# Experts of a mixture-of-experts stage in pairs, with high and low pieces stacked as rows of one stationary operand

## The reference, cut to what matters

```
g_sel = argmax(g_logits)                  # one of 4 groups a token
top_v, top_i = top_k(e_in, 2)             # two of its 8 experts
expert_idx = g_sel * 8 + top_i            # 256 * 2 = 512 assignments to 32 experts
hb = silu(xb @ w_g[e]) * (xb @ w_u[e])    # 1024 -> 512, twice
y = hb @ w_d[e]                           # 512 -> 1024
out[token] += y * gate
```

## Time and profile before

| what | value |
|---|---|
| median of 3 runs | 2004.26 us (2004.13 to 2004.6) |
| the profiled execution's own time | 2002.97 us |
| its span | 2001.2 us |
| PE busy | 1889.1 us (94%), 9124 matmuls |
| DVE busy | 1336.1 us (67%) |
| ACT busy | 1053.1 us (53%) |
| weights loaded by SP's queue | 423.87 MB in 400 transfers |
| experts' stage, from its first matmul to the last combining one | 257.9 to 858.3 us |

### The profile page before, as it was taken

The page is one execution under the profiler, slowest core; times in us unless marked ns, Lnnn a source line. Parts: engine busy times, 40 slices in busy tenths (PEclk is TensorE's granted clock), DMA queues, the critical chain, the costliest instruction groups (busy, mean ns, idle before and its releaser), DMA issues.

```text
span 2001.2 us, 22062 instructions
## 1 busy us (share of the span) xinstructions
PE 1889.1 (94%) x9124; PEld 1559.7 (78%) x9124; DVE 1336.1 (67%) x1263; ACT 1053.1 (53%) x1060; POOL 188.9 (9%) x171
## 2 busy tenths in 40 slices
PE   5998589999999999989999989999999999799998
PEld 4986467877787787768888978887888788587887
DVE  3776578888888888765546865555554668746554
ACT  3553367777877787644434354444443444335442
POOL 0001021111111110000000000000000108300000
PEclk9999789999999999989999999999999999899999
DMA  8744368999999999935546435555555667355551
GB/s 291 214 154 158 106 243 329 353 351 352 351 350 352 346 360 347 379 125 184 187 171 233 132 107 196 189 189 177 191 189 189 218 217 240 104 188 194 182 185 60
DMA packets 76219, 454.53 MB, mean 227 GB/s; under 512 B 16582, under 2 KB 17030, under 8 KB 24785
## 3 DMA queue, kind: packets, MB, share of 16 engines
q1 hardware_dynamic: 59024, 423.87, 58.3%
q0 software_dynamic: 16064, 27.51, 5.0%
q10 hardware_dynamic: 1024, 1.69, 0.3%
HBM read 461.49 MB, written 22.02 MB: 242 GB/s over the span
## 4 chain that ended last, share of the span: by engine, by line
PE 85%; DVE 7%; ACT 3%; POOL 2%; issue 2%; DMA 1%; SPq 0%; POOLq 0%; DVEq 0%; ACTq 0%
PE PS L422 27%; PE PS L424 26%; PE PS L423 26%; DVE wl L417 3%; ACT wh L408 2%; PE PS L1480 1%; PE PS L2013 1%; POOL vv L2633 1%; POOL vv L2635 1%; PE PS L1494 1%; DMA ring<-in_wt 1%; PE PS L2507 1%; DVE xg__148 L527 1%; DVE yTl L472 0%; PE PS L517 0%
## 5 line engine op out<-in xcount | busy, mean ns | idle before, releaser
L417 DVE TENSOR_TENSOR wl<-ring,wh 128x2048 fp32r<-128x2048 f32 x356 | 817.9, 2300 | 404.5 <-ACT wh L408 404.4
L408 ACT ACTIVATE wh<-ring 128x2048 fp32r<-128x2048 f32 x356 | 676.4, 1903 | 308.4 <-PE PS L424 307.0
L422 PE MATMUL PS<-wh,XTh 128*128 128x512 f32 x1048 | 418.3, 399 | 21.9 <-DVE wl L417 17.6
L424 PE MATMUL PS<-wh,XTl 128*128 128x512 f32 x1048 | 411.2, 392 | 0.0
L423 PE MATMUL PS<-wl,XTh 128*128 128x512 f32 x1048 | 411.1, 392 | 0.0
L422 PEld LDWEIGHTS PS<-wh,XTh 128*128 128x128 f32 x1048 | 198.8, 190 | 66.6 <-DVE wl L417 21.3
L424 PEld LDWEIGHTS PS<-wh,XTl 128*128 128x128 f32 x1048 | 198.5, 189 | 42.6
L423 PEld LDWEIGHTS PS<-wl,XTh 128*128 128x128 f32 x1048 | 198.9, 190 | 39.5
L422 PE MATMUL PS<-wh,xgT 128*128 128x512 f32 x388 | 159.1, 410 | 7.3 <-issue 2.9
L424 PE MATMUL PS<-wh,xgT 128*128 128x512 f32 x388 | 153.6, 396 | 0.0
L423 PE MATMUL PS<-wl,xgT 128*128 128x512 f32 x388 | 152.7, 394 | 0.0
(11 more groups left out here) (415 smaller groups left out, 2717.3 us busy)
## 6 DMA issues: line engine op xcount, KB each, us to landing
ring<-in_wt SPq DMA_DIRECT2D x400, 1024.0 KB, 5.1
xtmp<-in_norm_g POOLq DMA_DIRECT2D x6, 512.0 KB, 6.7
bb<-in_b_b_in POOLq DMA_DIRECT2D x12, 256.0 KB, 5.2
toep<-frow POOLq DMA_DIRECT2D x1, 2048.0 KB, 48.3
...
```

The lines of the kernel that those rows point to most:

```text
L408: s.activation(k.pieces(i)[0], k.raw(i), ACT.Copy).then_inc(*k.w_hi.up(i))
L417: v.tensor_tensor(l, k.raw(i), h.bitcast(F32), ALU.subtract).then_inc(*k.w_lo.up(i))
L422: pe.matmul(o, lhsT=left[0], rhs=right[0], start=first, stop=False)
L424: return pe.matmul(o, lhsT=left[1], rhs=right[0], start=False, stop=final)
```

## The change

Two experts share one gather of 64 + 64 tokens (`SEATS` = 64), one turning and one store. The turned tokens of an expert are laid out as 64 high columns and 64 low columns of one stationary operand, so that gate and up need two matmuls for each 128 rows of weights (by the high and by the low piece of the weights) where `three` took three: 32 an expert for 48. Rows 0 to 63 of the result hold the high tokens' product, rows 64 to 127 the low ones'. ACT copies the result to SBUF (`gs`, `us`), and four float32 matmuls of 64 moving columns with `fold` (two identities, one under the other) turn it and add its halves (`fold_gate`, `fold_up`). silu, the product `pr` and the pieces of h then have 256 columns for 512. The down product keeps three matmuls with 128 stationary columns, in which the other expert's 64 seats are zero, and both experts of a pair add up in the same PSUM banks (`down`, `rows`). The parts come in the order gate 0, gate 1, up 0, down 0, down 1 (of the expert before), up 1. Slots of a pair are made from ranks shifted by 512 for odd experts. `rest_*` now runs where an expert has over 64 tokens, in two rounds of 32.

```diff
     for e in range(32):
+        g = len(parts)
         cols("w_e_gate", (0, e), 0, 512)
+        u = len(parts)
+        cols("w_e_up", (0, e), 0, 512)
         if e:
             deep("w_e_down", (0, e - 1), 0, 4)
-        cols("w_e_up", (0, e), 0, 512)
+            parts.append(parts.pop(u + 1))
+            stage["down", e - 1] = (u + 1, u + 2)
+        stage["gate", e], stage["up", e] = (g, g + 1), (u, len(parts) - 1)
+    stage["down", 31] = (len(parts), len(parts) + 1)
     deep("w_e_down", (0, 31), 0, 4)
...
-        self.hsm = here("hsm", 8872, 512)
-        self.hrm = here("hrm", 9384, 512)
+        self.gs, self.us = here("gs", 8872, 512), here("us", 9384, 512)
+        self.sg, self.pr = here("sg", 9896, 256), here("pr", 10152, 256)
+        self.fold = here("fold", 10408, 64)
+        self.odp = here("odp", 8872, 4, 16)
...
-        self.xgT = [[here(f"xgT{x}{h}", 10672 + 2048 * x + 1024 * h, 8, 128, dtype=F32R) for h in T] for x in T]
+        self.xgT = [here(f"xgT{x}", 10672 + 2048 * x, 8, 2, 128, dtype=F32R) for x in T]
...
+    pe.wait_ge(*k.d["late"].at("late"))
     pe.wait_ge(*m.v.at("both"))
     for t in T:
+        pe.matmul(bank(0, 32, 32 * t), lhsT=k.ones, rhs=k.odd, start=True, stop=False)
...
-    def up_part(i, e, b, p):
+            for x in range(4):
+                o = 128 * (4 * q + x)
+                mm = pe.transpose(bank(6 + q, 128, 128 * x), k.xg[j % 2][:, o:o + 128], k.ident)
+            mm.then_inc(*m.pe.up(f"xt{j}.{q}g"))
+
+    def part(i, e, b, p):
         pe.wait_ge(*k.w_lo.at(i))
         w = k.weights(i)
         for j in range(4):
             kk = 4 * p + j
-            mm = rows_of(pe, bank(b), k.xgT[e % 2], kk, 0, w, j, 0, 512, kk == 0, kk == 7)
+            for n in T:
+                mm = pe.matmul(bank(b), lhsT=k.xgT[e // 2 % 2][:, kk, e % 2, :], rhs=w[n][:, j, :],
+                               start=(kk, n) == (0, 0), stop=(kk, n) == (7, 1))
         mm.then_inc(*k.w_used.up(i))
 
-    def turn_h(e):
-        pe.wait_ge(*m.v.at(f"pr{e}"))
+    def fold(src, b, name):
         for j in range(4):
-            mm = pe.transpose(bank(2, 128, 128 * j), k.hrm[:, 128 * j:128 * j + 128], k.ident)
-        mm.then_inc(*m.pe.up(f"ht{e}"))
-
-    def down(i, e, b):
+            mm = pe.matmul(bank(b, 64, 64 * j), lhsT=src[:, 128 * j:128 * j + 128], rhs=k.fold, start=True, stop=True)
+        mm.then_inc(*m.pe.up(name))
+
+    def fold_gate(e):
+        pe.wait_ge(*m.s.at(f"gs{e}"))
         if e:
-            pe.wait_ge(*m.s.at(f"yb{e - 1}"))
+            pe.wait_ge(*m.s.at(f"si{e - 1}"))
+        fold(k.gs, 2, f"fg{e}")
+
+    def fold_up(e):
+        pe.wait_ge(*m.s.at(f"us{e}"))
+        if e:
+            pe.wait_ge(*m.v.at(f"pr{e - 1}"))
+        fold(k.us, 3, f"fu{e}")
+
+    def down(e):
+
+        if e % 2 == 0 and e:
+            pe.wait_ge(*m.s.at(f"yb{e // 2 - 1}"))
         pe.wait_ge(*m.v.at(f"hl{e}"))
-        for p in range(2):
-            pe.wait_ge(*k.w_lo.at(i + p))
-            w = k.weights(i + p)
+        for p, i in enumerate(k.at["down", e]):
+            pe.wait_ge(*k.w_lo.at(i))
+            w = k.weights(i)
             for nn in range(2):
                 for j in range(2):
                     kk = 2 * p + j
-                    mm = rows_of(pe, bank(b + nn), k.hTm[e % 2], kk, 0, w, j, 512 * nn, 512 * nn + 512, kk == 0, kk == 3)
+                    mm = rows_of(pe, bank(4 + nn), k.hTm[e % 2], kk, 0, w, j, 512 * nn, 512 * nn + 512,
+                                 (e % 2, kk) == (0, 0), (e % 2, kk) == (1, 3))
                 if (e, p, nn) == (31, 1, 0):
                     mm.then_inc(*m.pe.up("y31"))
-            mm.then_inc(*k.w_used.up(i + p))
-
-    def combine(x, t, nn):
-        return pe.matmul(bank(4 + 2 * t + nn), lhsT=k.PT[:, x, 128 * t:128 * t + 128],
-                         rhs=k.yr[:, x, 512 * nn:512 * nn + 512], start=x == 0, stop=x == 1)
-
-    i = k.at["moe"]
+            mm.then_inc(*k.w_used.up(i))
+
     turn_x(0)
     for e in range(32):
+        g, u = k.at["gate", e], k.at["up", e]
+        if e % 2 == 0:
+            pe.wait_ge(*m.v.at(f"xl{e // 2}.1g"))
         if e:
-            pe.wait_ge(*m.s.at(f"si{e - 1}"))
-        pe.wait_ge(*m.v.at(f"xl{e}.1g"))
-        up_part(i, e, 0, 0)
+            pe.wait_ge(*m.s.at(f"gs{e - 1}"))
+        part(g[0], e, 0, 0)
         if e:
-            turn_h(e - 1)
-        up_part(i + 1, e, 0, 1)
-        i += 2
-        if e:
-            down(i, e - 1, 4)
-            i += 2
-            pe.wait_ge(*m.v.at(f"pr{e - 1}"))
+            fold_up(e - 1)
+        part(g[1], e, 0, 1)
         if e == 2:
             pe.wait_ge(*m.v.at("hotg"))
             for x in T:
                 for t in T:
-                    mm = pe.matmul(bank(3, 128, 256 * x + 128 * t), lhsT=k.ones, rhs=k.hotg[:, x, t, :], start=True,
+                    mm = pe.matmul(bank(6, 128, 256 * x + 128 * t), lhsT=k.ones, rhs=k.hotg[:, x, t, :], start=True,
                                    stop=True)
             mm.then_inc(*m.pe.up("gates"))
-        up_part(i, e, 1, 0)
-        if e < 31:
-            turn_x(e + 1)
-        up_part(i + 1, e, 1, 1)
-        i += 2
-    turn_h(31)
+        if e:
+            pe.wait_ge(*m.s.at(f"us{e - 1}"))
+        part(u[0], e, 1, 0)
+        if e:
+            down(e - 1)
+        if e % 2 and e < 31:
+            if e == 3:
+                pe.wait_ge(*m.v.at("PT1"))
+            turn_x(e // 2 + 1)
+        fold_gate(e)
+        part(u[1], e, 1, 1)
+    fold_up(31)
     pe.wait_ge(*m.v.at("PT1"))
-    pe.wait_ge(*m.s.at("yb30"))
-    for t in T:
-        for nn in T:
-            combine(0, t, nn)
-    down(i, 31, 2)
+    down(31)
     for t in T:
         for nn in T:
             if t == 0:
-                pe.wait_ge(*m.s.at(("ya31", "yb31")[nn]))
-            combine(1, t, nn).then_inc(*m.pe.up(f"c{t}.{nn}"))
+                pe.wait_ge(*m.s.at(("ya15", "yb15")[nn]))
+            pe.matmul(bank(COMBINED[2 * t + nn]), lhsT=k.PT[:, 128 * t:128 * t + 128],
+                      rhs=k.yr[:, 1, 512 * nn:512 * nn + 512], start=True, stop=True).then_inc(
+                *m.pe.up(f"c{t}.{nn}"))
...
+    def product(e):
+        v.wait_ge(*m.s.at(f"si{e}"))
+        v.wait_ge(*m.pe.at(f"fu{e}"))
+        if e:
+            v.wait_ge(*m.v.at(f"hl{e - 1}"))
+        v.tensor_tensor(k.pr, k.sg, bank(3, 256), ALU.mult).then_inc(*m.v.up(f"pr{e}"))
+
+    def low(e):
+        h, l = [seats(x, e) for x in k.hTm[e % 2]]
         v.wait_ge(*m.s.at(f"hh{e}"))
-        v.tensor_tensor(l, bank(2).rearrange("p (k i) -> p k i", k=4), h.bitcast(F32),
-                        ALU.subtract).then_inc(*m.v.up(f"hl{e}"))
-
-    i = k.at["moe"]
+        v.tensor_tensor(l, k.pr.rearrange("p (k i) -> p k i", k=4), h.bitcast(F32), ALU.subtract).then_inc(
+            *m.v.up(f"hl{e}"))
+
     turn_x(0)
     for e in range(32):
+        g, u = k.at["gate", e], k.at["up", e]
         if e:
-            turn_h(e - 1)
-        for n in range(4 if e else 2):
-            split_lo(v, k, k.after[i + n])
-        i += 4 if e else 2
-        if e < 31:
-            turn_x(e + 1)
-        split_lo(v, k, k.after[i])
-        v.wait_ge(*m.s.at(f"si{e}"))
-        v.wait_ge(*k.w_used.at(i + 1))
-        v.tensor_tensor(k.hrm, k.hsm, bank(1), ALU.mult).then_inc(*m.v.up(f"pr{e}"))
-        split_lo(v, k, k.after[i + 1])
-        i += 2
+            d = k.at["down", e - 1]
+            split_lo(v, k, k.after[k.at["up", e - 1][1]])
+            product(e - 1)
+        split_lo(v, k, k.after[g[0]])
+        if e:
+            low(e - 1)
+        split_lo(v, k, k.after[g[1]])
+        split_lo(v, k, k.after[u[0]])
+        if e:
+            for i in d:
+                split_lo(v, k, k.after[i])
+        if e % 2 and e < 31:
+            turn_x(e // 2 + 1)
+        if e == 0:
+            for h in T:
+                for x in T:
+                    v.memset(seats(k.hTm[x][h], 1 - x).bitcast(F32), 0.0).then_inc(*m.v.up(f"hz{x}{h}"))
+            v.wait_ge(*k.d["xn"].at("xn"))
+            v.memset(k.xg[1], 0.0).then_inc(*m.v.up("xz1"))
...
+    def gate(e):
+        s.wait_ge(*k.w_used.at(k.at["gate", e][1]))
+        if e:
+            s.wait_ge(*m.pe.at(f"fg{e - 1}"))
+        s.activation(k.gs, bank(0), ACT.Copy).then_inc(*m.s.up(f"gs{e}"))
+
+    def up(e):
+        s.wait_ge(*k.w_used.at(k.at["up", e][1]))
+        if e:
+            s.wait_ge(*m.pe.at(f"fu{e - 1}"))
+        s.activation(k.us, bank(1), ACT.Copy).then_inc(*m.s.up(f"us{e}"))
+
+    def silu(e):
+        s.wait_ge(*m.pe.at(f"fg{e}"))
+        if e:
+            s.wait_ge(*m.v.at(f"pr{e - 1}"))
+        s.activation(k.sg, bank(2, 256), ACT.Silu).then_inc(*m.s.up(f"si{e}"))
+
+    def high(e):
+        s.wait_ge(*m.v.at(f"pr{e}"))
+        if e >= 2:
+            s.wait_ge(*k.w_used.at(k.at["down", e - 2][1]))
+        s.activation(seats(k.hTm[e % 2][0], e), k.pr.rearrange("p (k i) -> p k i", k=4), ACT.Copy).then_inc(
             *m.s.up(f"hh{e}"))
 
```

(92 more changed lines are left out.)

255 lines of the change are left out of this document (110 added, 145 removed).

## The result

The changed kernel takes **1986.09 us** (median of 4 runs, 1984.77 to 1988.06) against 2004.43 for the kernel before in the same session; the ratio is 0.9906, with a 95% interval of 0.9889 to 0.9924. The forecast was 1992 with a range of 1966 to 2018. The profiled execution took 1984.77, its span is 1982.9.

What follows compares the result with a forecast made beforehand. PE was taken as the bound, DVE close behind. Loops -25, first loop -3, end 0 and clock falls +16 made -12 from 2002.97, so 1991; with the median 1.3 above that execution, forecast 1992 us, range 1966 to 2018.

Steps and rivals of the forecast that it cites:

- What bounds the kernel: Experts' stage before the change: PE is the bound at 18.28 us an expert, with DVE close behind.
- PE's own share: Experts' loops: PE's work falls to 15.0 us an expert, a fold costing 0.88; alone this would save some 86 us.
- The layout of the loop: Experts' loops laid out by hand: PE stalls of 2.05 and 2.22 us, a pair at 34.9 for 36.56, 25 us saved.
- The clock: Experts' loops: PE's clock falls behind one stall in three, at 1.6 us each, 16 us lost; bounds none and 48.
- the clock falls at most stalls: Rival, experts' loops: PE returns from most stalls at 1.2 GHz, 2024 us if at all; 0.26 that it ends slower.
- First loop and end: First expert loop 3 us less, between 0 and 5; end of the experts' stage 0, between -2 and +4.
- Ahead of the loop: nothing: Before the expert loops: two more float32 matmuls, about 0.9 us, are paid by two fills fewer on DVE; nothing.
- DMA: Experts' weight stream: costs nothing, as 421 GB/s gives 14.9 us an expert and no more than 17.4 is asked.
- The stream as a rival: Rival, experts' loops: weight transfers bind at 361 GB/s, 17.7 us an expert, 18 less, 1984 to 1990 us; chance 0.06.
- No stalls at all: Rival, experts' loops: DVE and ACT run ahead of the hand layout, 15.4 us an expert, 89 less, 1915; chance 0.06.

Runs made afterwards that it cites:

- With filling: Changed kernel plus three float32 matmuls of 256 columns, results unused, ahead of each of PE's two waits a pair; 1977.94 us.
- the version with h ahead: Changed kernel with the product and both pieces of h ahead of a weight part each on ScalarE and VectorE, instead of behind it; 1981.24 us.
- The version with both moves: Changed kernel with product and pieces of h ahead of the weight parts, and x turned ahead of the down parts, its pieces made earlier; 1934.30 us.

## Why the prediction held, and where it did not

- **What bounds the kernel, right.** PE before, and after the change none of the engines by its work, but the order in which ScalarE and VectorE hand on. Doubling the folds, moving the turning of x and moving the pieces of h showed it.
- **PE's own share, right.** A fold was to cost 0.88; its eight records take 1.00 from 573.76 to the last one's recorded end, some 0.9 by the distance of starts.
- **The layout of the loop, right in form and in size.** By starts, as the layout counts, the odd loop above has stalls of 1.8 and 2.2 us where 2.05 and 2.22 were laid out, and the even loop 0.25 before down 0 for 0.41. As recorded they are 1.6 to 1.7 and 1.9 for the forecast 1.9 and 2.0. A pair without a fall takes 34.6; the layout came to 34.7, and 34.9 was taken. The other side of the difference was too small: 36.56 for a pair of the kernel before is twice one distance of 18.28, and the mean from loop 1 to 29 is 36.8 (514.7 for 14). So the change is worth 2.1 a pair for the forecast 1.65. With filling, no falls and at least as much work, the 14 pairs take 485.9, 29 less than before, where 14 x 1.65 = 23 was forecast.
- **The clock, too dear.** One fall in three was forecast, 10 of 30, for 16 us. The first profile has 4 in the 14 pairs, behind the waits for x, at 1.2 us each, 4.7 in all. By the medians all falls together cost some 8. So the share was too high, and the price of 1.6, which came from the combining at the end of the stage, was somewhat too high as well. The rival "the clock falls at most stalls" did not come in this kernel, but it did in the version with h ahead, where 22 us went that way. The rival had the mechanism and the wrong condition. It counted stalls; what goes along with the falls is how long PE idles at once: none of 60 behind 1.6 to 1.7 us, 16 of 60 behind 1.9, 12 of 15 behind 2.4 to 3.5, and none where filling had cut the idle times to 0.6.
- **First loop and end.** -2.5 and -1.2 for -3 and 0.
- **"Ahead of the loop: nothing", wrong: +6.6.** This is the step that failed. The term counted two matmuls more and two fills less. It left out that `rest_*` doubled from 32 to 64 rounds, since no round is run. The two sizes, 32 and 64 rounds, with all else equal, show 6.6 us of the median. Why the first gather is issued later and lands later behind a longer jump was not tried. Loading of instructions is a guess that the traces speak for, with 7 packets of the instruction queue there for 5, but no run changes it alone.
- **Behind the stage, no term was put down, wrong by 2.9.** From the first scaling to the end of the span 7.2 us stand for 4.3. It is 7.2 to 7.3 in all eight profiles of the changed kernel and its versions with 64 rounds and 6.9 in the three with 32 or 4, so 0.3 of it goes with the overflow code. The kernel before with small overflow code took 4.3. The time lies behind the last byte of the output; its cause stays open.
- **DMA, right for this kernel.** No engine waits for the ring. The Trainium skill ("DMA: Bandwidth & Descriptors", the table of limits at its head) has HBM bind one core at about 358 GB/s. The trace doesn't agree: 401 to 416 GB/s in eight slices of 50 us from 350 us on in the version with both moves, and there it does bind. The Trainium skill ("HBM Reference", "Specifications (TRN2)") also says that a core streaming alone measures well above its share, since the figure is for two cores that stream at once. This kernel runs on one core, and with that sentence the trace agrees: it is the one that should have been weighed.
- **The stream as a rival (0.06), 1984 to 1990,** had a number near the measured one by chance: no engine waits for a part. Its rate was misread, too: the ten slices from 350 us on have a mean of 354 GB/s and not 361, by which it would have come out 8 us under the old time and not 18.
- **No stalls at all (0.06), 1915:** not in this kernel. The version with both moves got to 1934. The stream, which that rival had left out, bound its loops, and the 6.6 at the head and the 2.9 at the end are in its time as well.

The total came out right to 6 us in part by luck, since errors had opposite signs. By the marks of the two profiled executions 11 us too much were put down for the clock and 4 too little for what the loops gain, against 9.5 not seen at the head and the end.
